# Two decoder layers with NSA and differential attention: the layout of NSA's value matmuls, the place of its softmax scaling, and the order of work in the layer norm

## The reference

```python
u = x * (1.0 + sc1) + sh1
x = layer_norm(ALPHA * x + (1.0 + g1) * token_mixer(u), ln1_g, ln1_b)
u = x * (1.0 + sc2) + sh2
x = layer_norm(ALPHA * x + (1.0 + g2) * swiglu(u), ln2_g, ln2_b)
```

```python
out = gb[..., 0:1] * o_cmp + gb[..., 1:2] * o_sel + gb[..., 2:3] * o_win   # each o = softmax(scores) @ values
```

## Time and profile before

| what | value |
|---|---|
| median of 3 runs | 1799.22 us (1799.19 to 1803.18) |
| profiled execution | 1796.96 us, span of the trace 1795.1 us |
| mean granted TensorE clock | 0.986 of full speed |
| PE busy | 1700.7 us (95%), 8620 matmul records |
| DVE busy | 986.0 us (55%), 1516 instructions |
| ACT busy | 633.2 us (35%), 1146 instructions |
| DMA | 192.05 MB, mean 107 GB/s |

### The profile page before, as it was taken

One profiled execution on the slowest core, in us unless ns is written; L12 is line 12 of the kernel. 1 busy time (PEld: TensorE's weight loads), 2 busy tenths in 40 slices (PEclk: granted clock), 3 DMA queues, 4 the chain that ended last, 5 costly groups with the idle time before them and its releaser, 6 DMA issues.

```text
span 1795.1 us, 21919 instructions
## 1 busy us (share of the span) xinstructions
PE 1700.7 (95%) x8620; PEld 1382.5 (77%) x8620; DVE 986.0 (55%) x1516; ACT 633.2 (35%) x1146; POOL 51.2 (3%) x100
## 2 busy tenths in 40 slices
PE   6899899899999999999989998899999999999997
PEld 5778667677787888888878776677777788888886
DVE  4776555656676555554557655555576633333344
ACT  0532344444334322222243324444452533222222
POOL 2000000000000000000000000000000000000000
PEclk9999999999999999999999999999999999999997
DMA  9554221113525666655426231100223233333331
GB/s 319 150 170 129 72 58 48 41 43 112 146 83 152 187 187 184 184 166 154 146 68 170 82 83 36 36 24 24 59 83 94 59 102 97 95 103 90 97 97 47
DMA packets 269686, 192.05 MB, mean 107 GB/s; under 512 B 8169, under 2 KB 254481, under 8 KB 268561
## 3 DMA queue, kind: packets, MB, share of 16 engines
q1 hardware_dynamic: 255632, 147.94, 28.2%
q0 software_dynamic: 12032, 42.07, 7.8%
q10 hardware_dynamic: 1920, 0.66, 0.2%
HBM read 188.54 MB, written 2.10 MB: 106 GB/s over the span
## 4 chain that ended last, share of the span: by engine, by line
PE 83%; DVE 7%; ACT 5%; issue 3%; DMA 2%; SPq 0%; ACTq 0%; DVEq 0%
PE banks L1463 22%; PE banks L1465 21%; PE banks L1464 21%; PE banks L1579 4%; PE banks L1613 3%; ACT probs L801 3%; PE banks L1638 3%; DVE w_lo L895 1%; DMA ring<-in_w_in_dram 1%; PE banks L1512 1%; PE banks L1514 1%; PE banks L1513 1%; PE banks L1581 1%; DMA ada_first_a<-in_w_ada_dram 1%; PE banks L1527 1%
## 5 line engine op out<-in xcount | busy, mean ns | idle before, releaser
L1463 PE MATMUL banks<-u_hi,w_hi 128*128 128x512 f32 x1216 | 499.2, 411 | 13.2 <-DVE w_lo L895 7.8
L1465 PE MATMUL banks<-u_hi,w_lo 128*128 128x512 f32 x1216 | 475.6, 391 | 0.0
L1464 PE MATMUL banks<-u_lo,w_hi 128*128 128x512 f32 x1216 | 475.4, 391 | 0.0
L895 DVE TENSOR_TENSOR w_lo<-ring,w_hi 128x1024 fp32r<-128x1024 f32 (+2 forms) x246 | 294.4, 1199 | 325.3 <-ACT w_hi L633 324.7
L633 ACT ACTIVATE w_hi<-ring 128x1024 fp32r<-128x1024 f32 (+2 forms) x246 | 253.7, 1032 | 230.3 <-PE banks L1465 102.2
L1463 PEld LDWEIGHTS banks<-u_hi,w_hi 128*128 128x128 f32 x1216 | 229.8, 189 | 55.2 <-DVE w_lo L895 9.5
L1465 PEld LDWEIGHTS banks<-u_hi,w_lo 128*128 128x128 f32 x1216 | 228.9, 188 | 49.5
L1464 PEld LDWEIGHTS banks<-u_lo,w_hi 128*128 128x128 f32 x1216 | 230.1, 189 | 36.9
L1463 PE MATMUL banks<-h_hi,w_hi 128*128 128x512 f32 x352 | 138.5, 394 | 0.0
L1465 PE MATMUL banks<-h_hi,w_lo 128*128 128x512 f32 x352 | 137.0, 389 | 0.0
L1464 PE MATMUL banks<-h_lo,w_hi 128*128 128x512 f32 x352 | 137.0, 389 | 0.0
(11 more groups left out here) (228 smaller groups left out, 2107.3 us busy)
## 6 DMA issues: line engine op xcount, KB each, us to landing
ring<-in_w_ffn_in_dram SPq DMA_DIRECT2D x88, 512.0 KB, 3.9
ada_ring<-in_w_ada_dram POOLq DMA_DIRECT2D x80, 512.0 KB, 4.3
ring<-in_w_in_dram SPq DMA_DIRECT2D x72, 512.0 KB, 3.8
ring<-in_w_ffn_out_dram SPq DMA_DIRECT2D x32, 448.0 KB, 3.6
ring<-in_w_out_dram SPq DMA_DIRECT2D x16, 512.0 KB, 3.9
ring<-in_w_ffn_out_dram SPq DMA_DIRECT2D x16, 512.0 KB, 4.1
ada_first_a<-in_w_ada_dram SPq DMA_DIRECT2D x5, 1024.0 KB, 9.5
w<-in_cmp_w_k_dram SPq DMA_DIRECT2D x8, 512.0 KB, 4.9
```

The source lines that it names most:

```text
L895: V.tensor_tensor(lo, src, hi.bitcast(fp32), ALU.subtract).then_inc(split_lo, 1)
L1463: M(bank, wh[:, block], sh[:, k, :], start=start, stop=False)
L1464: M(bank, wh[:, block], sl[:, k, :], start=False, stop=False)
L1465: return M(bank, wl[:, block], sh[:, k, :], start=False, stop=stop)
```

## The change

NSA's values become the stationary operand and the transposed probabilities move, so the output comes out transposed: two heads on the two halves of the partitions, 128 tokens as columns. For that the probabilities are scaled by gate over sum on VectorE before they are transposed, and the three branches add up in one PSUM bank, which ScalarE copies to `q_rot` once a tile, at step 12. Step 13, the scaling of output banks and the additions go; the differential heads get the other bank. All steps now wait on `mix_done` before the transposes. In the layer norm the column sums of the squares move ahead of those of the last block, the spreads become transposes, six filler products before and one behind them go (nine become eight), the fold moves behind 1/std, and `unshift` moves ahead of the weight split. The functions that count semaphores follow. Cut to its core:

```diff
--- before.py
+++ after.py
@@ gate_units, ADA_STEPS, SEQUENCE, turned_by_act
-    n, steps = GM_IN * KD, TT * (STEPS + 1)
+    n, steps = GM_IN * KD, TT * STEPS
-ADA_STEPS = {4 + 7 * k: k for k in range(KD)}
+ADA_STEPS = {3 + 6 * k: k for k in range(KD)}
-SEQUENCE = [(i, j) for i in range(TT) for j in range(STEPS + 1)]
+SEQUENCE = [(i, j) for i in range(TT) for j in range(STEPS)]
...
@@ scalar engine, attention loop
-                            if j == STEPS:
-                                nc.scalar.activation(
-                                    q_rot[:, :, i * P:(i + 1) * P],
-                                    turned[:, 0, :].rearrange("p (c t) -> p c t", c=4), ACT.Copy)\
-                                    .then_inc(turn_act, 1)
...
+                    if t >= 4 and SEQUENCE[t - 4][1] == 8:
+                        i = SEQUENCE[t - 4][0]
+                        act.wait_ge(nsa_done, l * TT + i + 1)
+                        nc.scalar.activation(q_rot[:, :, i * P:(i + 1) * P],
+                                             nsa_ps.rearrange("p (c t) -> p c t", c=4), ACT.Copy)\
+                            .then_inc(nsa_saved, 1)
...
@@ vector engine, layernorm
                 for m in range(KD):
+                    if m >= 2:
+                        link(unshift(m))
                     prepare_behind(l, names[m])
...
-                    if m >= 2:
-                        link(unshift(m))
...
-                if which == 0:
-                    ada_part2(l)
-                elif l + 1 < DEPTH:
-                    ada_part1(l + 1)
                 mean_s, var_s, rstd_s, square_s = (ln_s[:, k, :] for k in (0, 2, 3, 1))
...
                 V.reciprocal(rstd_s, var_s).then_inc(rstd_saved, 1)
+                if which == 0:
+                    ada_part2(l)
+                elif l + 1 < DEPTH:
+                    ada_part1(l + 1)
@@ vector engine, attention loop
-                for t in range(len(SEQUENCE) + 2):
+                for t in range(len(SEQUENCE) + 3):
                     if 1 <= t <= len(SEQUENCE):
...
-                        if 9 <= j < STEPS:
-
-                            dve.wait_ge(exp_done, s + 1)
+                        dve.wait_ge(exp_done, s + 1)
+                        if j == 0:
+                            p_all = probs[:, s % 2, 0, 0:256].rearrange("p (h n) -> p h n", n=NCP)
+                            link(V.tensor_reduce(sums[:, i % 2, 0:8], p_all, AX.X, ALU.add))
+                            link(V.reciprocal(coef[:, 0, :], sums[:, i % 2, 0:8]))
...
+                            link(V.tensor_tensor(coef[:, 0, :], coef[:, 0, :], gates[:, i, :, 0], ALU.mult))
+                            V.tensor_tensor(p_all, p_all, coef[:, 0, :].unsqueeze(2).to_broadcast([P, 8, NCP]),
+                                            ALU.mult).then_inc(mix_done, 1)
+                        elif j <= 8:
+                            br, c = (j - 1) // 4, (j - 1) % 4
+                            at = 8 + 2 * (j - 1)
+                            link(V.reciprocal(coef[:, 1, 0:2], sums[:, i % 2, at:at + 2]))
+                            for h in range(2):
+                                last = V.tensor_scalar(probs[:, s % 2, h, 0:N], probs[:, s % 2, h, 0:N],
+                                                       coef[:, 1, h:h + 1], gates[:, i, 2 * c + h, br + 1:br + 2],
+                                                       ALU.mult, ALU.mult)
+                            last.then_inc(mix_done, 1)
+                        else:
                             hd = j - 9
...
-                    if t >= 2:
-                        i, j = SEQUENCE[t - 2]
-                        if j in (0, 4, 8, 12):
...
-                                link(V.tensor_tensor(
-                                    dst[:, :].rearrange("p (h d) -> p h d", d=HEAD_DIM),
-                                    bank.rearrange("p (h d) -> p h d", d=HEAD_DIM),
-                                    coef[:, 0, :].unsqueeze(2).to_broadcast([P, 8, HEAD_DIM]), ALU.mult))
...
-                                    ins = V.tensor_tensor(o_nsa[:, :], o_nsa[:, :], t1, ALU.add)
...
+                    if 2 <= t < len(SEQUENCE) + 2 and SEQUENCE[t - 2][1] == 12:
...
+                        link(V.tensor_tensor(od, diff_ps.rearrange("p (h e) -> p h e", h=4),
+                                             d_rs[:, 0, :].unsqueeze(2).to_broadcast([P, 4, P]), ALU.mult))
...
+                    if t >= 3 and SEQUENCE[t - 3][1] == 12:
...
+                        link(V.tensor_tensor(sq, od, od, ALU.mult))
+                        ins = V.tensor_reduce(d_sq[:, 4 * i:4 * i + 4], sq, AX.X, ALU.add)
...
@@ tensor engine, turn and values
-                if j < STEPS:
-                    pe.wait_ge(exp_done, s + 1)
-                if 9 <= j < STEPS:
-                    pe.wait_ge(mix_done, (l * TT + i) * 4 + j - 8)
-                if j == STEPS:
-                    pe.wait_ge(nsa_ready, l * TT + i + 1)
-                    blocks = [(0, c, o_nsa[:, c * P:(c + 1) * P]) for c in range(4)]
-                elif j == 0:
+                pe.wait_ge(mix_done, s + 1)
+                if j == 0:
...
-                if j in (0, 1, 5, 9) and q >= 2:
-
-                    pe.wait_ge(out_saved, q - 1)
+                s, done_before = score_step(l, i, j), l * TT + i
+                if j == 0 and done_before:
+
+                    pe.wait_ge(nsa_saved, done_before)
+                elif j == 9 and done_before:
+                    pe.wait_ge(out_saved, done_before)
...
-                    for g in range(2):
-                        last = M(bank[:, 256 * g:256 * (g + 1)], probsT[:, s % 2, 0, g * P:(g + 1) * P],
-                                 v_cmp[:, g, :], start=True, stop=True)
+                    for c in range(4):
+                        g, cols = c // 2, slice(P * (c % 2), P * (c % 2 + 1))
+                        last = M(nsa_ps[:, c * P:(c + 1) * P], v_cmp[:, g, cols],
+                                 probsT[:, s % 2, 0, g * P:(g + 1) * P], start=c == 0, stop=False,
+                                 skip_group_check=True)
...
-                    for h in range(2):
-                        head = 2 * c + h
-                        v = slice(128 * br + 64 * (c // 2), 128 * br + 64 * (c // 2) + 64)
-                        for b in range(i + 1):
-                            last = M(bank[:, 64 * head:64 * head + 64], probsT[:, s % 2, h, b * P:(b + 1) * P],
-                                     v_tok[:, b, v], start=b == 0, stop=b == i)
+                    v = slice(128 * br + 64 * (c // 2), 128 * br + 64 * (c // 2) + 64)
+                    for b in range(i + 1):
+                        for h in range(2):
+                            last = M(nsa_ps[64 * h:64 * h + 64, c * P:(c + 1) * P], v_tok[:, b, v],
+                                     probsT[:, s % 2, h, b * P:(b + 1) * P], start=False, stop=br == 1 and b == i,
+                                     skip_group_check=True)
...
-                if j in (0, 4, 8, 12):
-
-                    last.then_inc(out_done, 1)
-                    pe.wait_ge(out_done, q + 1)
+                if j in (8, 12):
+
+                    done_now = nsa_done if j == 8 else out_done
+                    last.then_inc(done_now, 1)
+                    pe.wait_ge(done_now, done_before + 1)
                     pe.sem_inc(pv_done, 1)
...
@@ tensor engine, mean_and_variance
-                        ins = M(out[:, i * P:(i + 1) * P], ln_s[:, k, i:i + 1].to_broadcast([P, P]), ident,
-                                start=True, stop=True)
+                        ins = nc.tensor.transpose(out[:, i * P:(i + 1) * P], ln_s[:, k, i:i + 1].to_broadcast([P, P]),
+                                                  ident)
...
                 columns(mean_col, t2, True, False)
+                pe.wait_ge(sq_summed, n + 1)
+                columns(var_col, squares[:, 0, :], True, False)
                 wait_saved(pe, l, ("wo", "fo")[which] + str(KD - 1))
                 columns(mean_col, res[:, KD - 1, :], False, True).then_inc(mean_done, 1)
-                pe.wait_ge(sq_summed, n + 1)
-                columns(var_col, squares[:, 0, :], True, False)
                 pe.wait_ge(squared, (n + 1) * KD)
                 columns(var_col, squares[:, KD - 1, :], False, True).then_inc(var_done, 1)
-                keep_busy(2)
                 pe.wait_ge(mean_saved, n + 1)
                 spread(mean_ps, 0).then_inc(mean_spread, 1)
-                keep_busy(4)
                 pe.wait_ge(rstd_saved, n + 1)
                 spread(rstd_ps, 3).then_inc(rstd_spread, 1)
                 if n + 1 < 2 * DEPTH:
-                    keep_busy(9)
+                    keep_busy(8)
```

132 lines of the change are left out of this document (50 added, 82 removed).

## The result

The changed kernel takes **1761.26 us** (median of 4 runs, 1761.2 to 1762.05) beside 1800.51 for the kernel before in the same sitting (4 runs, 1799.19 to 1803.18): a ratio of 0.978 (95% interval 0.9764 to 0.9795), 39.2 us less. By the spans of the profiled executions it is 1795.1 - 1759.4 = 35.7 us less. The forecast was 1758, with 1748 to 1778 around it.

The account below looks back on a forecast made before the run. The prediction took a ring of waits to bound the attention loop. Attention 28.6 (33.2 - 4.6) plus norms 13.0 made 41.6 us less: 1755.4 profiled, 1757.6 against the median, stated as 1758, range 1748 to 1778.

Parts of the forecast that it names:

- the ring: Attention loop: score, gate unit, transposes, ScalarE's copy, two exponentials set each step: 2.75, 3.50, 4.24, 4.99 us in tiles 0 to 3.
- The fourteenth step: Attention tiles: the step that transposed the summed output goes, leaving 13 turns a tile; 16.6 us less a layer, 33.2 in all.
- the sum: Whole kernel: attention 28.6 plus norms 13.0 makes 41.6 us less, 1755.4 for the profiled execution.
- the pile-ups: Attention: VectorE's queue delays scaling and transposes in first steps of tiles and where adaLN slices meet splits; 4.6 us lost.
- what is late next: Attention: the term for delays where VectorE's queue piles up; 4.6 us taken, bounds 0 and 10.2.
- Value matmuls: Attention loop, TensorE: 80 ns each taken, bounds 55 to 161, from 108; tile 3 needs 1.3 us in place of 1.73.
- the two-unit steps: Attention steps with two merge-gate units, where TensorE itself is later: 5.56 us in tile 3, coming down to about the ring.
- rival 2: Attention loop: value matmuls get dearer; 1784 us at 161 ns, 1766 at 108 ns; chance 0.07.
- Scaling at nothing: Attention, VectorE: scaling probabilities before the transposes costs nothing, hidden by scores and one gate unit; ready after 1.3 us in tile 3.
- Norms: Four layer norms: 1/std earlier, its first multiplication sooner, fewer fillers; 13.0 us less, bounds 9 to 14.
- Rival 4: Attention loop: lighter TensorE work lets the clock fall to 1.2 GHz, making the kernel slower, up to 1836 us; chance 0.04.

Follow-up runs that it names:

- The doubled run: The changed kernel with every value matmul of the selected and window branches issued twice: 1782.75 us, ratio 0.9882.
- the norm's part alone: The kernel before with only the layer norm changes: 1787.34 us, ratio 0.9914.
- the few value matmuls: The kernel before with value matmuls of the selected and window branches for the last key block alone, 384 of 640 left out: 1791.75 us, ratio 0.994.

## Why the prediction was right, and where it was off

**The bound and the mechanism: right, but for tile 0.** The loop is a ring. The chain of the kernel after, in tile 3 (start, length, count), is the ring itself, and no value matmul is in it:

```profile
361.64 0.89 PE banks L1584 x8
...
362.55 0.02 ACT probsT L771
...
363.05 1.45 ACT probs L796 x4
...
364.54 1.13 PE banks L1556 x4
```

It is so in tiles 1 and 2 too. In tile 0 it is not: there the value matmuls hold 10% of the chain (from 197 to 223 us) and the exponentials 6%, and most scores show no wait for an exponential, which the prediction had named as a sign:

```profile
205.59 0.37 PE banks L1610 x4
205.96 0.49 PE banks L1556 x4
```

The steps of tile 0 have the ring's 2.74 us with one gate unit and with two, so two bounds, the ring and TensorE's own work, nearly coincide there (the slack of 0.07 us above). That the prediction's length held for both kinds of step in tile 0 was partly luck.

Otherwise the steps came out at the lengths that were read from before; taking 41 us of value work away gave 11; moving one gate unit gave 20 with no work removed. The fourteenth step of each tile went.

**The number: nearer than the sum.** For the profiled execution the sum gave 1755.4 us, and 1761.2 was measured, 5.8 more. The forecast of 1758 added the 2.3 us by which the median of before lay above its profiled execution; in the kernel after the two are the same (1761.2 and 1761.26). So part of the closeness is luck.

**The fourteenth step, 33.2 us, and the pile-ups, 4.6: the sum was 5 to 6 us too good.** Attention gave about 23, the lower end of 23 to 35, in place of 28.6. In the trace of after, the steps that are longer than the ring are the first two of a tile and the last (and, by up to 0.17 us, the one before it in tiles 0 and 1). Over both layers the first two cost 8.9 us: 2.5 where a slice meets a tile's start in layer 0 (tiles 1 and 2), 0.7 from a lower clock in tile 0 of layer 0, the rest in both layers alike. The last differential step costs 0.47 us more in each of the 8 tiles, 3.8 in all. The prediction costed that at nothing: it said that ScalarE's copy of the sum moves to another bank "once a tile as before". ScalarE in tile 3 shows where it went:

```profile
386.23 0.60 ACT L771 ACTIVATE probsT<-banks 128x512 f32<-128x512 f32 x1 [2.63 <-PE banks L1584]
386.72 0.59 ACT L776 ACTIVATE q_rot<-banks 128x512 f32<-128x512 f32 x1
387.19 0.69 ACT L796 ACTIVATE probs<-banks,neg_max 128x512 f32<-128x512 f32 x1
```

It stands between the copy of the transposed block and the next exponential, so it is a link of the ring. Against these 12.7 us stand some 3 that the passages between tiles and the ends of the loops gave back. What remains is 10.0: the loops were to take 196.8 us each before "what is late next", and took 202.8 and 200.9, where about 199 had been named as the sign. For that term 4.6 was taken and 10.2 was the bound; it was too small, and one place, ScalarE's copy, was missed.

**Value matmuls: right in sum, wrong in parts.** 80 ns were taken between 55 and 161; they take 55, the lower bound, plus some 0.15 us for each group of them. In tile 3 the prediction had 1.3 us and the trace has 1.40 from the first value matmul to the next scores, 0.30 of it waiting. The halves do share time, as the row of the hidden layer had suggested, and that takes a matmul from 109 to 55 ns. The rule of the Trainium skill that was set against this row (TensorE: Matmul & The Clock Gate, Part 3), on weight loads, would have left no gain as the prediction read it; by the runs it does not hold for these column halves, and the table of measured speedups in the same Part, which has column tiles gain too, agrees with the runs. The Trainium skill's remark on the drain when the tiling mode changes (TensorEngine Tiling (Array Packing), Key Properties) would fit the 0.15 us that each step got dearer, though no run separates the change of mode from other causes.

**The text undervalued this part.** It held that at 108 ns only the two-unit steps would suffer, some 8 us. The doubled run, at nearly the time of before, lost 21.5: with the extra 0.15 us a step the slack of the two-unit steps is 0.07 us in tile 0 and 0.37 in tile 3, so a dearer matmul shows at once. By the same reasoning rival 2's 1784 us for 161 ns was too low; that was not run.

**Scaling at nothing: right in the steps.** Ready 1.2 us after the scores begin, and 0.75 before the transposes. In the whole trace the transposes wait 4.8 us for the scaled probabilities. Of its 51.6 us of VectorE's time 2.6 (medians) to 6.7 (spans) could be had back, and the steps that shortened are at the starts of tiles.

**Norms: right.** 13.5 us where 13.0 were forecast, and 1.25 us from 1/std to the first multiplication where 1.0 to 1.3 were named. The clock was taken at no cost. It was not quite that simple: in the first two norms the stretch at half the clock moved from the spreads onto the eight fillers behind them, where it costs nothing, and those eight are just what keeps it off the products. In the third it still lay on the last column sums and the spreads, which is the 0.2 us by which that norm is longer (8.95).

**Rival 4, the clock in the loop: no threat, but there.** The opening of the loop in layer 0, in the kernel after and in the kernel before (same columns as above):

```profile
190.00:193.40 3.40, 2.90 (x12) 2.28 (x13) 1.79 (x7) 2.17 (x6) 0.00 (x0) 0.59 0.00 0
```

```profile
190.00:193.40 3.40, 3.13 (x21) 2.27 (x22) 2.17 (x4) 1.97 (x6) 0.00 (x0) 1.00 0.00 0
```

Here the first step takes 3.99 us in place of 3.26 in layer 1. The profiled executions of nine of the twelve experiments show it in the same place, two of them for twice as long. Two of the nine (the norm's part alone, the few value matmuls) were built on the kernel before, in which the profiled execution had it not. It costs 0.6 to 2.4 us by the first two steps, and since it comes with either kernel it is no price of the change. Another stretch may be one: at the end of a loop TensorE ran the last sixteen value matmuls at half the clock (3.1 to 3.6 us in place of 2.01) in one layer of the kernel after and of six of the ten experiments with its loop, behind an idle time of 2.25 us in the kernel after, and in none of the three profiled executions with the loop of before, where that idle time was 1.07. It costs 1.1 to 1.6 us; no run separates its cause.

## What to carry to other kernels

In a loop written out over several engines, first find the ring: the instructions, each released by the one before, that lead back to the same instruction one step later. Work outside it costs only what exceeds its slack (41 us of work left out gave 11, 51.6 us gave 3 to 7), and an instruction queued in front of a link is part of it (20 us from the order of two calls, 3.8 from one copy in ScalarE's queue). Keep fillers only behind the last instruction that somebody waits for, and check by a run without them that they are needed.

## What the runs showed of the hardware that was not expected

- Records of fp32 matmuls with 128x64 stationary and 128 moving columns follow each other after 109 ns on one column half, and the other half runs beside it, 7 ns behind: 55 ns each. With 128x128 stationary and 64 moving columns they were 112 ns apart, so half as many moving columns had made nothing cheaper.
- The second half need not be interleaved to run beside the first: in the run with one head after the other, eight records (four and four) took the same 0.66 us as in alternation, and in groups of twelve and sixteen about four on each side overlapped where the heads meet.
- A group of them costs some 0.15 us beyond that, in a stream of 128x128 products.
- In the run without fillers the clock fell right behind the spread of the first norm (517.5) and TensorE, after 3.60 us of idleness, ran seven products at 1.2 GHz (0.43 us apart) before it was back at 2.4 (0.23). In the kernel after, eight fillers right behind the spread took 3.36 us, most of it at the lower level, and the first real products ran at full rate.
- A multiplication by two per-partition scalars takes 0.344 us for 128 columns and 0.544 for 512: by these two, 0.28 us of the small one's time, four fifths, is there whatever its width.
